# Where a token tile's expert queries and routes stand in the hand-written order of a fused layer kernel

## What is computed

```python
qv = (xi @ wq).reshape(B, PEER_BLOCK, PEER_HEADS, 2, half)
s = jnp.einsum('bthpc,hpnc->bthpn', qv, sub_keys)
top_s, top_i = lax.top_k(s, K)                       # K = 16, for each half of the key
cand_s = top_s[..., 0, :, None] + top_s[..., 1, None, :]
best_s, best_j = lax.top_k(cand_s, K)                # the best 16 of 256 pairs
gate = jax.nn.softmax(best_s, axis=-1)
act = gelu(einsum('btd,bthkd->bthk', xi, u_tab[expert]))
return einsum('bthk,bthkd->btd', gate * act, v_tab[expert])
```

## Time and profile before

| what | value |
|---|---|
| median of 3 runs | 2823.6 us (2821.54 to 2828.5) |
| span of the profiled execution | 2818.2 us |
| its own time beside the span | not given; the median is 5.4 us above the span |
| TensorE busy | 2309.7 us (82% of the span) |
| VectorE busy | 1353.8 us (48%) |
| ScalarE busy | 1299.6 us (46%) |
| GpSimd busy | 742.4 us (26%) |
| moved by DMA | 839.32 MB, of it 536.90 MB by the gather queue |

### The profile page before, as it was taken

How to read it: one execution, slowest core, us unless ns; L and a number is a source line. 1 busy time by engine, 2 the same in 40 slices (tenths; PEclk the granted TensorE clock), 3 DMA queues, 4 the chain that set the end, 5 groups by cost and what they waited for, 6 DMA issues and landing times.

```text
span 2818.2 us, 33729 instructions
## 1 busy us (share of the span) xinstructions
PE 2309.7 (82%) x13336; PEld 1955.2 (69%) x13336; DVE 1353.8 (48%) x3183; ACT 1299.6 (46%) x2327; POOL 742.4 (26%) x614
## 2 busy tenths in 40 slices
PE   7989998999999995887876877787788787666666
PEld 6878887876875875776755866666777675565554
DVE  3552333321002234666456765545766545686444
ACT  2751113100000212577745576844658764566665
POOL 0021112200000001233333323333323333334554
PEclk9989999999999997999996999898799899776665
DMA  5321211133434666999999999999999999999997
GB/s 241 117 90 60 78 65 45 53 138 144 151 150 156 253 236 258 421 408 416 399 421 403 411 421 419 408 421 421 390 420 410 414 383 420 393 365 363 417 421 311
DMA packets 109998, 839.32 MB, mean 298 GB/s; under 512 B 12176, under 2 KB 12432, under 8 KB 13968
## 3 DMA queue, kind: packets, MB, share of 16 engines
q0 software_dynamic: 73728, 536.90, 46.6%
q1 hardware_dynamic: 36112, 300.25, 27.0%
HBM read 836.06 MB, written 1.05 MB: 297 GB/s over the span
## 4 chain that ended last, share of the span: by engine, by line
PE 48%; DMA 24%; DVE 12%; ACT 10%; issue 4%; POOL 2%; SPq 0%; POOLq 0%; DVEq 0%; ACTq 0%
DMA mem<-in_puv,mem 23%; PE psm L442 11%; PE psm L2246 6%; PE psm L450 5%; DVE mem L2290 4%; PE psm L755 4%; PE psm L1809 4%; ACT mem L2264 3%; PE psm L2121 3%; PE psm L1350 3%; PE psm L1453 2%; PE psm L2008 2%; ACT L2259 1%; PE psm L1501 1%; PE psm L446 1%
## 5 line engine op out<-in xcount | busy, mean ns | idle before, releaser
L2246 PE MATMUL psm<-mem 128*128 128x128 f32 x4096 | 682.1, 322 | 363.6 <-ACT mem L2264 361.2
L2274 POOL DMA_INDIRECT mem<-in_puv,mem x512 | 621.1, 1213 | 1059.9 <-PE psm L2246 993.3
L2246 PEld LDWEIGHTS psm<-mem 128*128 128x128 f32 x4096 | 566.5, 167 | 475.7 <-ACT mem L2264 459.8
L2290 DVE CUSTOM_DVE_ANT_0 mem<-mem 128x1024 f32<-128x1024 f32 x512 | 624.5, 1225 | 471.3 <-DMA mem<-in_puv,mem 470.8
L2264 ACT ACTIVATE mem<-mem 128x1024 f32<-128x1024 f32 x512 | 588.8, 1150 | 16.7
L442 PE MATMUL psm<-mem 128*128 128x256 f32 (+2 forms) x1376 | 313.0, 390 | 3.1 <-DVE mem L1290 1.5
L2259 ACT ACTIVATE mem<-mem 128x1 f32<-128x1 f32 x512 | 101.9, 199 | 437.7 <-DVE mem L2290 434.5
L442 PEld LDWEIGHTS psm<-mem 128*128 128x128 f32 x1376 | 261.8, 192 | 53.2 <-issue 14.8
L1809 PE MATMUL psm<-mem 128*128 128x256 f32 x1024 | 256.0, 398 | 0.5 <-ACT mem L1529 0.5
L450 PEld LDWEIGHTS psm<-mem 128*128 128x128 f32 x1440 | 187.2, 196 | 49.1 <-issue 21.4
L450 PE MATMUL psm<-mem 128*128 128x128 f32 x1440 | 199.3, 283 | 22.6 <-DVE mem L1125 6.8
(11 more groups left out here) (364 smaller groups left out, 2365.7 us busy)
## 6 DMA issues: line engine op xcount, KB each, us to landing
mem<-in_w2g SPq DMA_DIRECT2D x64, 1024.0 KB
mem<-in_w SPq DMA_DIRECT2D x18, 2048.0 KB, 8.2
mem<-in_pwq SPq DMA_DIRECT2D x32, 1024.0 KB
mem<-in_w2f SPq DMA_DIRECT2D x28, 1024.0 KB
mem<-in_wgu SPq DMA_DIRECT2D x11, 2048.0 KB, 7.7
mem<-in_w2t SPq DMA_DIRECT2D x20, 1024.0 KB
mem<-in_w2b SPq DMA_DIRECT2D x16, 1024.0 KB
mem<-in_w2o SPq DMA_DIRECT2D x16, 1024.0 KB
```

Source lines behind the costliest of these rows:

```text
L2246: m = pe.matmul(bank(6 + c // 4)[:, tsl(c % 4)], GR[n % PING][:, 1024 + c * 128:1152 + c * 128], ident, is_transpose=True, start=k == 0 an ...
L2274: po.indirect_dma_start(GR[n % PING], None, A[f"puv{i // 2}"], bass.IndirectOffsetOnAxis(ap=IX[i % 2][:, k:k + 1], axis=0)).then_inc(gsem[ ...
L2290: ve.tensor_tensor_reduce(out=GR[n % PING][:, 0:1024], in0=GR[n % PING][:, 0:1024], in1=X[:, i % 2, :], scale=1.0, scalar=0.0, op0=MUL, op ...
```

## The change

It changes the list and nothing else. EARLY names the tiles whose query and route lie as a whole, all four chunks, at the end of the stretch beside the preceding tile's experts: tile 3 alone. For this tile, 16 of its 32 gates steps are put ahead of the weaving of gates, nsa and core. For tiles 0 to 2 the three own chunks are spread over 28 expert positions in place of 33. The order of SyncE's loads follows the list. Every instruction of the kernel is still there, once, with the same operands.

```diff
--- before.py
+++ after.py
@@ -257,10 +257,13 @@
         NE = 512
         weight = dict(fm=1.06, ht1=1.5, tm=1.7, gates=1.7, nsa=1.2, core=1.5, mix=1.5, query=1.06, route=0.7, fin=1.0)
 
+        EARLY = (3,)
+
         def tile_steps(i):
             front = ["fm"] * 28 + ["ht1"] * (i == 0) + ["tm"] * 4 + weave([("tm", 10, 1), ("core", 7, 0.7)])
-            attend = weave([("gates", 32, 1), ("nsa", 23, 1), ("core", 14, 0.7)])
-            return front + attend + ["mix"] * 24 + ["query"] * 8 + ["route"] * 20
+            ahead = 16 * (i in EARLY and i - 1 not in EARLY)
+            attend = ["gates"] * ahead + weave([("gates", 32 - ahead, 1), ("nsa", 23, 1), ("core", 14, 0.7)])
+            return front + attend + ["mix"] * 24 + (["query"] * 8 + ["route"] * 20) * (4 if i in EARLY else 1)
 
         plan = [(s, 0) for s in tile_steps(0)[:-36]]
         plan += [(s, 0) for s in tile_steps(0)[-36:]]
@@ -273,10 +276,11 @@
                 placed_at.append((128.0 * i + 1.5 + 118 * done / total if i < 3 else 128.0 * i + 1.5 + done, s))
                 done += weight[s[0]]
             lane = []
-            for c in R3:
-                lane += [("query", i)] * 8 + [("route", i)] * 20
+            lane = []
+            if i not in EARLY:
+                lane = ([("query", i)] * 8 + [("route", i)] * 20) * 3
             for n, s in enumerate(lane):
-                placed_at.append((128.0 * i + 0.2 + 33.0 * n / len(lane), s))
+                placed_at.append((128.0 * i + 0.2 + 28.0 * n / len(lane), s))
             plan += [s for _, s in sorted(placed_at, key=lambda x: x[0])]
         plan += [("e", NE), ("e", NE + 1)] + [("fin", 3)] * 12
```

## The result

The changed kernel takes 2866.7 us (median of 4 runs, 2864.26 to 2875.52), the one before 2822.6 us (median of 4). The ratio on record is 1.0168, 95% interval 1.0146 to 1.0190. The changed kernel is slower by 44 us between the medians, on the side that the forecast named, and outside its range of 2812 to 2849.

A forecast was written before the change was run, and what follows sets the result against it. The prediction took DMA bytes to bound the kernel's second half, the change affecting only lost rate: -21.3 + 27.1 + 4 + 0 = +9.8 us on the 2818.2 span, 2828.0; as median 2833.4 us (+0.35%), range 2812 to 2849.

The forecast's parts named there:

- The last tile: Tile 3's own experts, then without query or route: -21.3 us of lost rate, stretch from 346.6 to about 322 us.
- The four early chunks: Tile 3's chunks behind mix, beside tile 2's experts: +27.1 us of lost rate, bounds 12.8 and 39.6.
- The cycle of 33.3 us: Early chunk of tile 3: route phase 21.8 us plus query phase 11.5, for 9 experts with 22.4 us of bytes.
- Rival 1: Early chunks, 340 to 376: late weight loads keep them fed, four lose under 12.8 us; 2815 or 2811; chance 0.22.
- Rival 2: Early chunks' query phase shrinks, starts 28 us apart, 2822.5 us, no change; within the 0.28 given to 0.3%.
- The tighter stretch: Tile 3's nsa and core beside 29 of tile 2's experts, not 44: +4 us, between -4 and +12.
- The 16 gates steps put ahead lie where experts and gates have bytes enough: Before tile 3's nsa and core: 19 pieces, 47 us of bytes, stand beside the early gates.
- the bound of -4: Tighter stretch, best case: the early gates cure half of today's 8.9 us loss there.
- Rival 3: nsa and core in 29 experts lose the whole 8 to 12 us: 2837 to 2842, up to 2850; chance 0.14.
- The 28 positions: Own chunks of tiles 0 to 2 closer together: 0 us, since bytes still cover VectorE's cycle.
- the cover failed: Tiles 0 to 2: if 37 us of bytes do not cover the chunk cycle, some 2 us for each of three tiles.
- 15 + 7 x 1.14 + 12 = 35 us of VectorE's cycle: Chunk cycle of tile 2 at 28 positions: top-16 work, experts and query phase, against 37 us of bytes.

The follow-up runs named there:

- r5: Kernel before, with tile 3's steps beside tile 2's experts tightened as in the changed kernel, 16 gates ahead, only chunk 0 early: ratio 1.0061 to before.
- r3: Changed kernel without the 16 gates steps put ahead: ratio 1.0096 to the kernel before, tile 2 at 494.7 us.
- r9: Kernel before, with only 16 gates steps of tile 3 put ahead of nsa and core: ratio 1.0044 to before, tile 2 at 467.5 us.
- r1: Kernel before, with only the own chunks of tiles 0 to 2 over 28 expert positions in place of 33: ratio 1.0054 to before.
- r2: Changed kernel with 33 positions in place of 28 for the own chunks of tiles 0 to 2: ratio 1.0087 to the kernel before.

## Why the prediction was wrong

**The last tile** was right. It was to fall to about 322 us, and measured 322.2, at 421 GB/s from 2560 on. What stood there before was lost rate and three pieces of bytes, as said. The Trainium skill ("DMA: Bandwidth & Descriptors", Specifications) gives about 358 GB/s as a core's limit from HBM, its half of what two cores share; this program ran on one core, and its 280 us at 421 GB/s lie above that figure. The prediction's sum went by the measured rate.

**The four early chunks** were sized at 27.1 us, and measured 33.8. By chunk, the route phase and what follows it up to the next route phase (for chunk 3, up to 2520 us), by the windows above:

| chunk | predicted | measured | cycle |
|---|---|---|---|
| 0 | 5.9 | 0.0 + 3.5 | 32.8 us |
| 1 | 5.9 | 1.2 + 4.5 | 32.9 us |
| 2 | 8.4 | 3.8 + 7.8 | 36.5 us |
| 3 | 6.9 | 6.0 + 7.0 | - |

The cycle of 33.3 us, made from 15.0 us of top-16 work, a query phase of 11.5 and 1.14 us an expert, held for the first two. By the third, the experts themselves come late: TensorE has done 8 of the 64 query matmuls of chunk 3 when it stands 4.58 us for ScalarE's scaling of an expert, and VectorE then stands 10.87 us for S1.

```profile
2461.27 1.92 PE L2125 MATMUL psm<-mem 128*128 128x128 f32 x8
...
2467.76 1.97 PE L2250 MATMUL psm<-mem 128*128 128x128 f32 x8 [4.58 <-ACT mem L2268]
```

And chunk 3's loss does not end with its route phase. GpSimd waits 7.01 us for a buffer there, and then issues six gathers within 8 us:

```profile
2506.40 1.72 POOL L2278 DMA_INDIRECT mem<-in_puv,mem  x1 [7.01 <-PE psm L2250]
```

The mechanism was right, the sum 7 us short: the losses of chunks 2 and 3 were put at 8.4 and 6.9 us and measured 11.6 and 13.0, and those of chunks 0 and 1 came out at or under their price. Rival 1 is excluded, since the four lost 33.8 us and not under 12.8. Rival 2 is excluded too, since the chunks start 33 to 36 us apart and not 28.

**The tighter stretch** was put at +4 us with a bound of +12. Measured in the changed kernel it loses 22.3 us in 2142 to 2330 where the comparable window before (2127 to 2300) lost 9.5, so +12.9, and alone (r5) it costs 18.7 us. The step that failed is "The 16 gates steps put ahead lie where experts and gates have bytes enough", and with it the bound of -4 by which they might have helped. Asked was only whether the place that they went to has bytes enough. Not asked was what the place that they left then lives on, and how much room the chains keep: r3 and r9 put 13 us on the move, most of the term. What is left without it, +2 in r3's window (11.6 against 9.5) or 5.7 between r5 and r9, is about the +4 of the forecast. The working had 17 us of loss for this stretch, 8 more than before, and halved the 8 with an argument ("some of those waits were spent while experts were late anyway") for which no row stood. Rival 3 was the nearest of the four: its sign came (over 15 us in nsa's window), its time, up to 2850, was still too low, and its cause, nsa and core behind each other in 29 experts, is not parted from the missing gate loads.

**The 28 positions** were priced at 0, with 2 us a tile if the cover failed. They cost 7.3 and 7.5 us in tiles 0 and 1, and by themselves 6 to 8 in each of three tiles (r1, by the medians and by its profile). The step that failed is "15 + 7 x 1.14 + 12 = 35 us of VectorE's cycle". The 12 us of query phase came from the last tile, where TensorE has nothing but the query and experts. In tiles 0 to 2 it also has the next tile's projections, and the rows of the kernel before show the phase at 16.9 us there (the gates written at 1590.09, the next chunk's start at 1607.02). With 15 to 19 us the cycle is 38 to 42 us, longer than its 37 us of bytes; the one that was measured, 1613.21 to 1653.98, took 40.8. The price of a failed cover, "some 2 us for each of three tiles", was too low as well.

**The balance.** Tiles 0 and 1: +14.8, from the 28 positions. Tile 2: +53.2, of which 47.6 us are lost rate (62.7 against 15.1) and the rest, 5.6, is near the 7.5 us of bytes that come over from tile 3. Of the lost rate, 3.4 us are new in the first 120 us (5.7 against 2.3), 12.9 in the attention stretch, and 31 from 2330 on (34.4 against 3.4), where the four chunks lie. Tile 3: -24.4. The forecast had +9.8 for the whole, 33.8 too little: 15 for the 28 positions, 9 for the attention stretch, 7 for the chunks, and 3 for the start of tile 2, which it had at nothing. Those 3 us do not come from the 28 positions alone, since r2 loses as much there with 33. The side was right by the mechanism that the forecast named, the four chunks without loads beside them; the two terms that it held to be small, 4 and 0, carry most of the miss.

## What to carry to other kernels

When transfers bound a kernel, count the lost rate window by window, and ask of every part of an order which bytes stand beside it: work that holds the gathers up belongs where other loads are due, or must be spread until its own time and that of its experts fit into the time of their bytes, here 20 to 26 experts to a chunk. A step moved ahead leaves a hole behind it, and the hole has to be priced as well as the place it goes to. A phase's length holds only with the neighbours that it was measured beside.

## What the runs showed of the hardware

Gathers of 8 KB rows alone reach 421 GB/s over 280 us in the changed kernel, the rate that gathers and weight loads reach together in the earlier trace rows. And TensorE's granted clock was 0.63 in that stretch, against 0.88 and 0.87 beside the experts of tiles 0 and 1, without a cost that shows: the stretch lost no rate, and the last tile's 128 experts took 322 us, where their bytes alone need 319.
